# Moving a block of on-chip tiles 64 bytes up in a one-core RWKV-7 and pooling trunk

## The reference

```python
r = xr @ w_r ; k = xk @ w_k ; v = xv @ w_v              # 2048 x 2048 each
decay, a, g                                             # small two-stage projections, widths 96, 96 and 256
S = S * w_t + Sa * b_t + v_t * k_t ; y = S r_t          # per head of 64, along the tokens
x = LN(ALPHA * x + (y * g) @ w_o)
x = LN(ALPHA * x + (silu(x @ w_gate) * (x @ w_up)) @ w_down)
# layer 1: pooled differences d, then d @ w_grp (4 groups of 512 x 512), scale, LN, SwiGLU, LN
```

## Time and profile before

| what | value |
|---|---|
| median of 3 runs | 2808.06 us (2807.6 to 2808.61) |
| profiled execution, first to last instruction | 2809.2 us |
| TensorE matmul busy | 2701.7 us (96%) |
| TensorE weight load busy (beside the matmuls) | 2559.4 us (91%) |
| VectorE busy | 1598.3 us (57%) |
| ScalarE busy | 1143.2 us (41%) |
| GpSimd busy | 143.4 us (5%) |
| mean granted TensorE clock | 0.982 of full speed |
| DMA | 379.59 MB, mean 135 GB/s |

### The profile page before, as it was taken

How to read it: one execution, slowest core, us unless ns; L and a number is a source line. 1 busy time by engine, 2 the same in 40 slices (tenths; PEclk the granted TensorE clock), 3 DMA queues, 4 the chain that set the end, 5 groups by cost and what they waited for, 6 DMA issues and landing times.

```text
span 2809.2 us, 59165 instructions
## 1 busy us (share of the span) xinstructions
PE 2701.7 (96%) x24713; PEld 2559.4 (91%) x24713; DVE 1598.3 (57%) x2393; ACT 1143.2 (41%) x1628; POOL 143.4 (5%) x211
## 2 busy tenths in 40 slices
PE   7989999999999989999999999978999999999997
PEld 6978888888878889999999999967999999999997
DVE  7876777777775564444444444486444444444446
ACT  4564454454452353333333333345333333333334
POOL 1000111110100110000000000000000000000000
PEclk9999999999999999999999999989999999999999
DMA  8522222222223565565566654533565456555553
GB/s 230 149 80 61 76 65 65 73 66 64 73 85 88 165 166 165 164 165 148 165 184 167 166 167 141 166 124 86 166 167 164 140 166 189 164 164 164 148 165 96
DMA packets 707061, 379.59 MB, mean 135 GB/s; under 512 B 16023, under 2 KB 699191, under 8 KB 706711
## 3 DMA queue, kind: packets, MB, share of 16 engines
q1 hardware_dynamic: 701040, 363.54, 46.0%
q0 software_dynamic: 5792, 13.34, 2.0%
q10 hardware_dynamic: 70, 0.39, 0.1%
HBM read 367.39 MB, written 10.62 MB: 135 GB/s over the span
## 4 chain that ended last, share of the span: by engine, by line
PE 84%; DVE 11%; ACT 3%; issue 2%; DMA 0%; DVEq 0%; SPq 0%; POOL 0%; ACTq 0%
PE PS L711 24%; PE PS L712 23%; PE PS L713 23%; PE PS L861 4%; DVE WL L1693 2%; ACT WH L1264 1%; PE PS L913 1%; DVE TM L1837 1%; DVE TM L1825 1%; DVE PL L1795 1%; DVE TM L1701 1%; DVE ML L1708 1%; PE PS L985 1%; PE PS L885 1%; PE PS L728 0%
## 5 line engine op out<-in xcount | busy, mean ns | idle before, releaser
L1693 DVE TENSOR_TENSOR WL<-RAW,WH 128x2048 fp32r<-128x2048 f32 (+1 forms) x325 | 658.8, 2027 | 763.5 <-ACT WH L1264 763.5
L711 PE MATMUL PS<-MH,WH 128*128 128x288 f32 (+1 forms) x3152 | 933.2, 296 | 24.8 <-DVE ML L2077 11.1
L712 PE MATMUL PS<-ML,WH 128*128 128x288 f32 (+1 forms) x3152 | 934.8, 297 | 0.0
L713 PE MATMUL PS<-MH,WL 128*128 128x288 f32 (+1 forms) x3152 | 933.8, 296 | 0.0
L1264 ACT ACTIVATE WH<-RAW 128x2048 fp32r<-128x2048 f32 (+1 forms) x325 | 553.4, 1703 | 822.0 <-PE PS L713 807.7
L711 PEld LDWEIGHTS PS<-MH,WH 128*128 128x128 f32 (+1 forms) x3152 | 596.4, 189 | 30.9 <-issue 19.5
L712 PEld LDWEIGHTS PS<-ML,WH 128*128 128x128 f32 (+1 forms) x3152 | 596.6, 189 | 0.2
L713 PEld LDWEIGHTS PS<-MH,WL 128*128 128x128 f32 (+1 forms) x3152 | 596.1, 189 | 0.0
L712 PE MATMUL PS<-HL,WH 128*128 128x288 f32 x1408 | 415.3, 295 | 0.0
L713 PE MATMUL PS<-HH,WL 128*128 128x288 f32 x1408 | 415.0, 295 | 0.0
L711 PE MATMUL PS<-HH,WH 128*128 128x288 f32 x1408 | 413.4, 294 | 0.0
(11 more groups left out here) (324 smaller groups left out, 2909.4 us busy)
## 6 DMA issues: line engine op xcount, KB each, us to landing
RAW<-in_ffn_w_in SPq DMA_DIRECT2D x176, 1024.0 KB, 5.7
RAW<-in_ffn_w_down SPq DMA_DIRECT2D x128, 704.0 KB, 4.7
RAW<-in_rw_wr SPq DMA_DIRECT2D x16, 1024.0 KB, 5.9
PR<-in_rw_wk SPq DMA_DIRECT2D x64, 256.0 KB, 2.8
PR<-in_rw_wv SPq DMA_DIRECT2D x64, 256.0 KB, 3.0
PR<-in_rw_wo SPq DMA_DIRECT2D x64, 256.0 KB, 3.2
S0N<-in_state_wkv POOLq DMA_DIRECT2D x64, 64.0 KB, 2.4
out<-SOS POOLq DMA_DIRECT2D x64, 64.0 KB, 2.2
```

Of the source, the lines that this page charges most:

```text
L711: pe.matmul(out, wh, xh, start=first, stop=False)
L712: pe.matmul(out, wh, xl, start=False, stop=False)
L713: return pe.matmul(out, wl, xh, start=False, stop=last)
L1693: dve.tensor_tensor(WL[0:rows, j % 2, 0:n], RAW[0:rows, j, 0:n], WH[0:rows, j % 2, 0:n].bitcast(F32), ALU.subtract).then_inc(lo_ready, 1)
```

## The change

The offset of `XPS` grows by 64 bytes. All tiles that are placed behind it, directly or over one another, lie 64 bytes higher on each partition. `RAW`, `WH`, `WL`, `X` and the ring at offset 0 stay where they are. No instruction, wait, size or order is changed.

```diff
         X = at("X", [P, KC, T + 1], F32, after("WL"))
-        XPS = at("XPS", [P, KC, NS], F32, after("X"))
+        XPS = at("XPS", [P, KC, NS], F32, after("X") + 64)
         PAR = at("PAR", [P, 3 * P], F32, after("XPS"))
```

## The result

The changed kernel took 2823.63 us (median) against 2809.03 us for the kernel before in the same comparison, a ratio of 1.0046 with a 95% interval of [1.0037, 1.0055]. One of the 20 runs of the changed kernel took 8836.52 us and has no part in the ratio; the quotient of the two medians is 1.0052, inside the interval. The forecast of no change was wrong. The rival in which the two reads meet gave 2823 us.

A forecast was written before the change was run, and what follows sets the result against it. TensorE was taken to bound the kernel, busy for 96% of the span, through the fp32r matmul step in the SwiGLU stretches. All terms summed to 0 against the profiled 2809.2 us, giving 2808 us, range 2656 to 2825.

The forecast's parts named there:

- the two reads meet: From first SwiGLU slab: rows and WH weights coinciding within 128 bytes cost 1.1 ns per matmul, +15.2 us, 2823 us; chance 0.23.
- the decisive term: Moved rows against unmoved WH weights, 13,680 matmuls: taken as 0, bounded at 15.2 us either way.
- the 12 ns: Fp32r matmul step at full clock, 132.2 ns against 120 for the columns; the extra looked like a pause per instruction.
- the nearest row: Trace comparison by weights' place: 132.2 ns with WH at multiples of 128 bytes, 133.3 with W3H 64 past.
- Each operand pays for its own place: Rival: WH matmuls gain 1.1 ns, the others 2.2; 21 us faster, 2787 us, or 2794 with half; chance 0.15.
- The cut line: Rival: aligned rows touch 9 stretches of 128 bytes, not 10; step falls to 121.7 ns, -148 us, 2660 us; chance 0.17.
- The parts costed at nothing: VectorE and ScalarE on moved tiles, DMAs into moved tiles, and weights in PH, RH and W3H: each taken as 0.

The follow-up runs named there:

- e1: Kernel before with WH and all behind it 64 bytes higher: weights in WH 64 past a multiple of 128, moving rows at a multiple; 2808.54 us, ratio 0.9998.
- e2: Kernel before with WH and WL moved 64 bytes, rows left as there: weights in WH and rows both 64 past a multiple of 128; 2824.59 us, ratio 1.0054.
- e15: Changed kernel's layout, with 32 instead of 128 weight columns loaded in all but the first and last channel blocks of the SwiGLU stages; 2795.3 us, one run.
- e5: Kernel before with all tiles from XPS on 96 bytes higher: moving rows 32 past a multiple of 128, WH weights at 0; 2834.99 us, one run.
- e16: Kernel before with low weights WL alone moved to 64 past a multiple of 128, high weights at 0, rows at 64; 2801.99 us, ratio 0.9974.
- e13: Against the kernel before, low weights moved to 64 past a multiple of 128 and moving rows to 0, high weights at 0; 2814.35 us.
- e14: Against the kernel before, low weights and moving rows moved to 96 past a multiple of 128, high weights at 0; 2809.27 us.

## Why the prediction was wrong

*The step that failed* is the decisive term, "Moving rows against weights in WH, which stay". I bounded it by the nearest row at 15.2 us in either direction and took 0, because the 12 ns looked like a pause that need not know addresses. Measured was its upper bound: 1.1 ns on each WH matmul, 14.6 us on the median. The sentence behind it was half right. Most of the 12 ns are indeed indifferent to these places (steps of 131.7 to 134.5 ns over all layouts with full loads), but the rest is not, and the earlier trace rows had already shown that. A comparison in the trace that differs by 1.1 ns for a difference of place should not have been answered with 0 for a term that is a change of place. The row could not give the sign: the rival of the relative place read 15.2 us of loss out of it, the rival of each operand's own place 15.2 us of gain and more. The changed kernel and e1 told them apart. That 2823.63 us lie in the outer range of 2656 to 2825 us says nothing for the sum, since that range was stretched over the rivals.

*The reads meet* gave place, price and time: from the first SwiGLU slab on, 133.3 ns in WH, 133.3 still in PH and W3H, 2823 us. The runs e1 and e2 bear out its core, that the relative place counts, and e15 that it goes with the width of the loads beside the rows. Two others refute its wording, that coincidence costs: 32 past is worse than 0 (e5), and one coinciding load in three is better than none (e16). Its price was one row carried over to another layout; it held there, and is no rule.

*Each operand pays for its own place* is refuted by e1 and e2. *The cut line* is refuted by the changed kernel itself: rows that begin at multiples of 128 still take 133.3 ns. Its equality of numbers (ten stretches of 128 bytes, 133.3 ns) was a coincidence. Its count was also a little short: outside the first stage and the recurrence there are 12,768 matmuls with weights in WH and 96 in W3H, 12,864 and not 12,704, which is worth under 2 us of its price.

*The parts costed at nothing* hold. VectorE's and ScalarE's durations are those of before, as these rows of the changed kernel show against the earlier trace rows:

```profile
L1693 DVE TENSOR_TENSOR WL<-RAW,WH 128x2048 fp32r<-128x2048 f32 x195 | 446.8, 2292 | 545.7 <-ACT WH L1264 545.7
L1264 ACT ACTIVATE WH<-RAW 128x2048 fp32r<-128x2048 f32 x195 | 373.4, 1915 | 469.7 <-PE PS L713 456.4 <-PEq L1237 10.7 <-DMA RAW<-in_ffn_w_in 2.6
L1357 ACT ACTIVATE PH<-PR 128x512 fp32r<-128x512 f32 x128 | 76.9, 626 | 33.4 <-PE PS L713 32.2 <-DMA PR<-in_rw_wv 0.5 <-DMA PR<-in_rw_wk 0.5
L1344 ACT ACTIVATE PH<-PR 128x512 fp32r<-128x512 f32 x72 | 43.6, 626 | 34.4 <-PE PS L713 29.8 <-DMA PR<-in_rw_wo 4.3 <-DMA PR<-in_rw_g 0.2
```

VectorE's difference still takes 2292 ns and the rounding 1915 and 626, and the waits for PR's DMAs went from 0.8 + 0.6 and 4.0 + 0.5 us to 0.5 + 0.5 and 4.3 + 0.2. The 8 ns between WL and W3L on VectorE are not a matter of these places: W3L now lies at multiples of 128 bytes and still takes 2284. The weights in PH and W3H kept their distance to the rows and their step, as costed. The float32 sums keep their 241.7 ns, with 1.45 us for three of them:

```profile
2795.85 0.65 PE L1118 MATMUL PS<-SUM,CP 128*128 128x288 f32 x2
...
2797.30 0.65 PE L1124 MATMUL PS<-SQS,CP 128*128 128x288 f32 x2
```

The Trainium skill ("TensorE: Matmul & The Clock Gate", Part 2, the step on LDWEIGHTS) has the weights come through a read port of their own, so that loading them takes nothing from the running matmul. For these fp32r matmuls the measurement differs, and it decides: the place of the weights to the rows is worth 133.3 against 132.2 ns.

What stays open is the rule behind the step. It is not a sum over the three distances, and it takes several values for one layout (132.2 and 132.7 in e13, 131.7 and 134.4 in e14). In the layouts of the kernel before, the changed one, e1 and e2 every stretch kept one value. So the runs show that the change's loss comes from the rows' place relative to the weights, and not why that place costs what it does. What the other 11 ns are was not found either.

## What to carry to other kernels

Where a dense stretch is bound by one instruction's step, a shift of a tile is not free: compare steps between starts for every operand placement that the trace already holds, and where such a row shows an effect of place, do not put a change of place at 0. What counts in fp32r matmuls here is the place of the weights relative to the moving rows, though not that alone, so a rule like "begin rows at multiples of 128 bytes" can cost time. A gap of 64 bytes between the high and the low weights is worth trying: it gave 0.26% here, with the rows 64 past the high weights. With the rows at the place of the high weights (e13) the same gap left 2814.35 us, above the kernel before; so it has to be timed.

## What the runs showed of the hardware

I had not expected the step of an fp32r matmul of 288 columns at full clock to come in a few fixed values, apart by one or two times 0.56 ns (131.7, 132.2, 132.7, 133.3, 134.4; for a block of three matmuls the unit is 1.67 ns), nor that a stretch of thousands of matmuls keeps one of them to its end while an equal stretch of the same launch keeps another. With loads of 32 columns instead of 128 the step falls by only 0.3 to 2.0 ns.
